# A two-layer mixture-of-experts trunk on one core: later gathers as transpositions by permutations, and the activations turned inside the next up product

## What is computed

```python
probs = softmax(t @ w_router)                    # 256 tokens, 16 experts in 4 groups of 4
# the best group by the sum of its two best scores; of that group the two best experts
gate = (one_hot(idx) * w).sum(1)                 # weight of each token for each expert, 14 of 16 zero
for e in range(16):
    g, u = split(t @ w_gu[e], 2)                 # 1024 -> 2 x 512
    out += gate[:, e] * ((silu(g) * u) @ w_down[e])   # 512 -> 1024
```

## Time and profile before

| | us |
|---|---|
| median of 3 runs | 721.49 (720.32 to 723.93) |
| profiled execution, its time | 720.53 |
| its span in the trace | 718.8 |
| TensorE busy | 678.9 |
| VectorE busy | 180.7 |
| ScalarE busy | 141.2 |
| GpSimd busy | 22.6 |

### The profile page before, as it was taken

How to read it: one execution, slowest core, us unless ns; L and a number is a source line. 1 busy time by engine, 2 the same in 40 slices (tenths; PEclk the granted TensorE clock), 3 DMA queues, 4 the chain that set the end, 5 groups by cost and what they waited for, 6 DMA issues and landing times.

```text
span 718.8 us, 7132 instructions
## 1 busy us (share of the span) xinstructions
PE 678.9 (94%) x2910; PEld 309.4 (43%) x2910; DVE 180.7 (25%) x452; ACT 141.2 (20%) x320; POOL 22.6 (3%) x41
## 2 busy tenths in 40 slices
PE   6999999999999999999989998999999999999983
PEld 5854564554343343433334455455333343343331
DVE  0010221460121121111135255553112112112125
ACT  1120360112121121211132051212111111121112
POOL 3200100000000000000000011200000000000000
PEclk9999999999999999999999999999999999999997
DMA  9999705145999999999999802650999999999921
GB/s 281 370 420 421 331 1 233 42 193 215 426 421 421 421 421 420 423 420 421 418 415 420 351 1 92 259 225 31 395 422 421 420 421 420 423 421 420 421 121 59
DMA packets 42165, 231.41 MB, mean 322 GB/s; under 512 B 8073, under 2 KB 12169, under 8 KB 16530
## 3 DMA queue, kind: packets, MB, share of 16 engines
q1 hardware_dynamic: 37696, 230.70, 78.4%
q10 hardware_dynamic: 4434, 0.21, 0.5%
HBM read 229.85 MB, written 1.05 MB: 321 GB/s over the span
## 4 chain that ended last, share of the span: by engine, by line
PE 88%; DVE 6%; ACT 3%; POOL 1%; ACTq 1%; issue 1%; POOLq 0%; DVEq 0%
PE pb L559 31%; PE pb L387 17%; PE pb L594 16%; PE pb L544 5%; PE pb L424 4%; PE pb L606 4%; PE pb L723 2%; PE pb L578 1%; PE pb L358 1%; PE pb L516 1%; PE pb L365 1%; DVE bufA L1255 1%; PE pb L525 1%; POOL bufA L339 1%; DVE bufA L1080 1%
## 5 line engine op out<-in xcount | busy, mean ns | idle before, releaser
L387 PE MATMUL pb<-ring,hT 128*128 128x512 f32 x320 | 141.3, 595 | 0.8 <-DVE hT L1409 0.8
L594 PE MATMUL pb<-ring,bufC 128*64 128x512 f32 x512 | 116.6, 597 | 7.2 <-DVE bufC L1246 7.2
L559 PE MATMUL pb<-ring,bufB 128*64 128x512 f32 x512 | 113.3, 595 | 1.9 <-DVE bufC L1242 1.9
L559 PE MATMUL pb<-ring,hT 128*64 128x512 f32 x512 | 113.0, 594 | 0.0
L387 PEld LDWEIGHTS pb<-ring,hT 128*128 128x128 f32 x320 | 59.5, 190 | 70.7 <-issue 68.7
L1255 DVE COPY bufA<-pb 32x512 f32<-32x512 f32 x64 | 43.7, 683 | 128.6 <-PE pb L594 128.1
L1242 DVE TENSOR_TENSOR bufC<-bufC,pb 128x256 f32<-128x256 f32 x32 | 13.5, 421 | 213.6 <-ACT bufC L953 213.6
L559 PEld LDWEIGHTS pb<-ring,hT 128*64 128x64 f32 x512 | 36.1, 137 | 69.7 <-issue 69.2
L594 PEld LDWEIGHTS pb<-ring,bufC 128*64 128x64 f32 x512 | 34.4, 136 | 73.3 <-issue 62.8
L559 PEld LDWEIGHTS pb<-ring,bufB 128*64 128x64 f32 x512 | 35.5, 137 | 70.3 <-issue 65.4
L947 ACT ACTIVATE bufA<-pb 32x512 f32<-32x512 f32 x64 | 37.7, 590 | 133.2 <-PE pb L594 132.8
(11 more groups left out here) (194 smaller groups left out, 410.6 us busy)
## 6 DMA issues: line engine op xcount, KB each, us to landing
ring<-in_w_gu SPq DMA_DIRECT2D x128, 1024.0 KB, 20.8
ring<-in_w_down SPq DMA_DIRECT2D x64, 1024.0 KB, 20.7
ring<-in_w_in_a SPq DMA_DIRECT2D x8, 1024.0 KB, 20.0
ring<-in_w_in_a SPq DMA_DIRECT2D x8, 512.0 KB, 10.5
ring<-in_w_out_a SPq DMA_DIRECT2D x4, 1024.0 KB, 18.9
ring<-in_w_q_b SPq DMA_DIRECT2D x4, 1024.0 KB, 23.9
ring<-in_w_out_b SPq DMA_DIRECT2D x4, 1024.0 KB, 23.6
ring<-in_w_kv_shared SPq DMA_DIRECT2D x2, 1024.0 KB, 27.6
```

What stands on the lines that cost most here:

```text
L387: last = mm(pb[bank][:, :], hT[:, k, t * P:(t + 1) * P], slot(i0 + k // 2)[0][:, k % 2, c * HALF:(c + 1) * HALF], start=k == 0, stop=k == ...
L559: last = mm(pb[0][c * 64:(c + 1) * 64, :].rearrange("p (a n) -> p a n", a=2), xe[m % 2][:, k, g * SLOTS:(g + 1) * SLOTS], slot(u_gu(l, u) ...
L594: last = mm(pb[2][c * 64:(c + 1) * 64, :], heT[:, j * P + hf * 64:j * P + (hf + 1) * 64], w[:, j, c * HALF:(c + 1) * HALF], start=(j, hf) ...
```

## The change

- In quads 2 to 4 a gather is four transpositions with the slot table in the place of the identity. The table is then a full permutation: `make_perm` compares lane numbers with a destination `dest` for every token of the tile, and a token that the quad does not have goes to one of the slots that nobody has. Its gate weight there is zero.
- `make_dest` computes the destinations, once a layer, after `count_rounds`; `route` saves the counts, capped at 32, for it. GpSimd fills three more constants. Some small tiles are joined in `misc`.
- `inner_T(u - 1)` is issued in the middle of `gate_up(u)`, before k = 4, and no longer after it; the last one of a layer stays behind the down product before it. On VectorE `take_T(u)` stands ahead of `times_up(u + 1)` instead of behind it.

```diff
-        ones = sb("ones", [P, 1])
+        misc = sb("misc", [P, 8])
+        ones, token_no, b_gate, extra_f = misc[:, 0:1], misc[:, 1:2], misc[0:GW, 2:3], misc[:, 4:8]
...
+        lane_no = sb("lane_no", [P, P])
+        block_no = sb("block_no", [P, EXPERTS])
+        count = st[:, 0:64]
+        d_free, d_sum, d_step, d_in = [st[:, 64 + 8 * n:72 + 8 * n].rearrange("p (m t) -> p m t", t=NT) for n in range(4)]
+        d_old = st[:, 128:160]
+        dest = sb("dest", [P, QUADS, NT])
...
-        NCONST = 8
+        NCONST = 11
...
             for t in range(NT):
                 nc.gpsimd.iota(slot_no[...]).then_inc(consts, 1)
+            nc.gpsimd.iota(lane_no[:, :], pattern=[[1, P]], ...).then_inc(consts, 1)
+            nc.gpsimd.iota(token_no[:, :], pattern=[[0, 1]], base=0, channel_multiplier=1, ...).then_inc(consts, 1)
+            nc.gpsimd.iota(block_no[:, :], pattern=[[BLOCK, GROUPS], [0, PER_GROUP]], ...).then_inc(consts, 1)
             nc.gpsimd.memset(w_gate, 0.0).then_inc(gate_zero, 1)
...
 def gather(m, f, bank=1):
-                        last = mm(pb[bank][:, (k % 4) * P:(k % 4 + 1) * P], rows_of(h, t, k),
-                                  pick[m % 2][:, t, :, :].rearrange("p e s -> p (e s)"), start=True, stop=True)
+                        to, table = pb[bank][:, (k % 4) * P:(k % 4 + 1) * P], pick[m % 2][:, t, :, :].rearrange("p e s -> p (e s)")
+                        if m:
+                            last = nc.tensor.transpose(to, rows_of(h, t, k), table)
+                        else:
+                            last = mm(to, rows_of(h, t, k), table, start=True, stop=True)
 def gate_up(u):
                     for k in range(KC):
+                        if u and k == 4:
+                            inner_T(u - 1)
...
                     gate_up(u + 1)
-                    inner_T(u)
                     if m:
                         scatter(m - 1)
                     down(u)
                     if more:
                         gather(m + 1, 0)
                     gate_up(u + 2)
-                    inner_T(u + 1)
                     if more:
                         gather(m + 1, 1)
                     down(u + 1)
                     if more:
                         gather(m + 1, 2)
                     gate_up(u + 3)
-                    inner_T(u + 2)
                     if more:
                         gather(m + 1, 3)
                     down(u + 2)
-                    inner_T(u + 3)
                     if more:
                         gate_up(u + 4)
                     else:
+                        inner_T(u + 3)
                         pe.wait_ge(x_sb, (Q0 + QUADS) * 4 - 3 * START)
                         bcast_row(1, 2 * l + 1, 0)
                     down(u + 3)
...
 def route(l):
                 V.reduce_max(extra_f[:, 0:1], pb[1][:, 32:64], AX_X)
+                V.tensor_scalar(count, pb[1][:, 0:64], float(BLOCK), None, ALU.min)
                 link(V.tensor_scalar(pt, r_a, 1.0, None, ALU.subtract))
...
+            def make_dest():
+                by_expert = lambda ap: ap.rearrange("p (t g i) -> p i t g", g=GROUPS, i=QUADS)
+                passed, total = by_expert(count[:, 0:32]), by_expert(count[:, 32:64])
+                pt = pos[:, :, :].rearrange("p e t -> p t e")
+                old = d_old.rearrange("p (t e) -> p t e", t=NT)
+                kept = r_a
+                V.tensor_reduce(d_sum, passed, AX_X, ALU.add)
+                V.tensor_tensor(old, pt, block_no[...], ALU.add)
+                link(V.scalar_tensor_tensor(out=kept, in0=kept, scalar=float(BLOCK), in1=oh, op0=ALU.is_le, op1=ALU.mult))
+                V.scalar_tensor_tensor(out=d_free, in0=total[:, :, :, 0], scalar=token_no[:, 0:1], in1=d_sum,
+                                       op0=ALU.add, op1=ALU.subtract)
+                link(V.tensor_tensor(old, old, kept, ALU.mult))
+                V.tensor_reduce(d_in, by_expert(d_old), AX_X, ALU.add)
+                for g in range(1, GROUPS):
+                    link(V.scalar_tensor_tensor(out=d_step, in0=d_free, scalar=float(g * BLOCK), in1=total[:, :, :, g],
+                                                op0=ALU.is_ge, op1=ALU.mult))
+                    link(V.tensor_tensor(d_free, d_free, d_step, ALU.add))
+                link(V.tensor_reduce(d_sum, by_expert(st[:, 96:128]), AX_X, ALU.add))
+                link(V.scalar_tensor_tensor(out=d_step, in0=d_sum, scalar=1.0, in1=d_free, op0=ALU.subtract, op1=ALU.mult))
+                link(V.tensor_tensor(dest[:, :, :], d_in, d_step, ALU.subtract))
+            def make_perm(m):
+                return V.tensor_tensor(pick[m % 2].rearrange("p t e s -> p t (e s)"),
+                                       lane_no[...].to_broadcast([P, NT, P]),
+                                       dest[:, m, :]...to_broadcast([P, NT, P]), ALU.is_equal)
...
                 make_pick(0).then_inc(pick_ready, 1)
                 count_rounds(l)
+                make_dest()
...
                     make_pickg(m).then_inc(pickg_ready, 1)
                     if more:
-                        make_pick(m + 1).then_inc(pick_ready, 1)
+                        make_perm(m + 1).then_inc(pick_ready, 1)
+                    take_T(u)
                     times_up(u + 1)
-                    take_T(u)
                     take_y(u)
+                    take_T(u + 1)
                     times_up(u + 2)
-                    take_T(u + 1)
                     take_y(u + 1)
+                    take_T(u + 2)
                     times_up(u + 3)
-                    take_T(u + 2)
                     take_y(u + 2)
                     take_T(u + 3)
```

More of the change, by code:

```diff
@@ L83, in build @@
         sink = sb("sink", [P, A_HEADS // 2])
-        b_gate = sb("b_gate", [GW, 1])
         cs = sb("cs", [P, NT, DH])
@@ L137, in build @@
         pos = sb("pos", [P, EXPERTS, NT])
+        lane_no = sb("lane_no", [P, P])
+        block_no = sb("block_no", [P, EXPERTS])
         gate = sb("gate", [P, EXPERTS, NT])
-        extra_f = sb("extra_f", [P, 4])
         extra = sb("extra", [P, 2], I32)
         ln = st[:, 0:40].rearrange("p (t n) -> p t n", t=NT)
+        count = st[:, 0:64]
+        d_free, d_sum, d_step, d_in = [st[:, 64 + 8 * n:72 + 8 * n].rearrange("p (m t) -> p m t", t=NT) for n in range(4)]
+        d_old = st[:, 128:160]
+        dest = sb("dest", [P, QUADS, NT])
         pb = [ctx.enter_context(nc.psum_tensor(f"pb{n}", [P, HALF], F32)) for n in range(8)]
@@ L308, in _ @@
                                allow_small_or_imprecise_dtypes=True).then_inc(consts, 1)
+            nc.gpsimd.iota(lane_no[:, :], pattern=[[1, P]], base=0, channel_multiplier=0,
+                           allow_small_or_imprecise_dtypes=True).then_inc(consts, 1)
+            nc.gpsimd.iota(token_no[:, :], pattern=[[0, 1]], base=0, channel_multiplier=1,
+                           allow_small_or_imprecise_dtypes=True).then_inc(consts, 1)
+            nc.gpsimd.iota(block_no[:, :], pattern=[[BLOCK, GROUPS], [0, PER_GROUP]], base=0, channel_multiplier=0,
+                           allow_small_or_imprecise_dtypes=True).then_inc(consts, 1)
             nc.gpsimd.memset(w_gate, 0.0).then_inc(gate_zero, 1)
@@ L1226, in of_quad @@
                         .rearrange("p t (g o) -> p t g o", o=1).to_broadcast([P, NT, 4, BLOCK]))
+            def make_dest():
[5 more added lines that the diff above has]
+                V.tensor_reduce(d_sum, passed, AX_X, ALU.add)
+                V.tensor_tensor(old, pt, block_no[:, :].rearrange("p (t e) -> p t e", t=1).to_broadcast([P, NT, EXPERTS]), ALU.add)
+                link(V.scalar_tensor_tensor(out=kept, in0=kept, scalar=float(BLOCK), in1=oh, op0=ALU.is_le, op1=ALU.mult))
[12 more added lines that the diff above has]
+                return V.tensor_tensor(pick[m % 2].rearrange("p t e s -> p t (e s)"),
+                                       lane_no[:, :].rearrange("p (t s) -> p t s", t=1).to_broadcast([P, NT, P]),
+                                       dest[:, m, :].rearrange("p (t o) -> p t o", o=1).to_broadcast([P, NT, P]), ALU.is_equal)
             def make_pick(m):
```

## The result

The changed kernel takes 713.0 us (median of 4 runs, 710.85 to 713.45) beside 721.42 for the kernel before: a ratio of 0.9863, 95% interval 0.9843 to 0.9883. The forecast was 712.3 (708.5 to 717.0). The profiled execution took 712.84, its span is 711.1.

A forecast was written before the change was run, and what follows sets the result against it. TensorE's own instructions were taken to bound the expert stages. Savings of 10.0 us over both layers, less 0.38 for the count and 0.45 for the start, gave -9.2: 721.49 to 712.3 us, range 708.5 to 717.0.

The forecast's parts named there:

- The bound: Expert stages: time is TensorE's own instructions and few waits; 88% of the last-ending chain is TensorE work, no DMA.
- six switches: Steady quad of 51.65 us: six changes between 64-column pairs and full 128-column work, 0.35 us each.
- Gathers: Quads 2 to 4: transpositions make a gather 0.48 us instead of 0.94, saving 0.46, 12 times a layer, 5.52 us.
- The move: Turning activations inside the next up product: loses nine shared switches a layer, costing 3.15 us, but hides copies.
- three better places: Moved turning where no gather fills the gap: first down product saves 0.91 us, quad 4 twice 0.86.
- Its reason: Turnings cannot stay behind their up product: a gather shortened by 0.46 us would only uncover VectorE's copy.
- The weights: Ring loads at layer 1's end lead by 9 to 11 us; 4 or more remain, no load late.
- VectorE's table: New slot table after the round count: 15 small operations, about 3 us, hidden in VectorE's idle time.
- The count: Capped count on VectorE ahead of the first gather's positions: not hidden, at most 0.19 us a layer, 0.38 in all.
- The start: GpSimd's three index fills delay ScalarE's first DMAs: 0.45 us, bounds 0 and 1.0.
- the dearer switch inside a product: Rival: a switch inside a running up product costs more, at 0.9 us giving 729 us; chance 0.05.
- The clock: Rival: TensorE's clock falls to half in the expert stages; four falls would give 719 us; chance 0.03.

The follow-up runs named there:

- e4: The changed kernel with turnings placed beside gathers or scatters where possible, only the first of a layer staying inside an up product; 706.8 us, ratio 0.9775.
- e5: e4 with the gathers' switches shared too, calls moved behind the scatter or beside turnings, none between an up and its down product; 705.0 us, ratio 0.9739.
- e7: The changed kernel with one more transposition inside each up product, issued before k = 2, so each is interrupted twice; 727.3 us, ratio 1.0049.
- e1: The changed kernel with gathers of quads 2 to 4 as plain matmuls again, turning still inside the next up product; 724.7 us, ratio 1.0019.
- e3: The changed kernel with the turning back behind its up product, keeping VectorE's new order, copy of turned activations ahead of the silu product; 711.5 us, ratio 0.9843.
- e8: The changed kernel with a weight ring of 18 slots in place of 22; 721.4 us, ratio 0.9962 to the kernel before.
- e6: e5 with GpSimd's three new constant fills moved behind the clearing that ScalarE's first DMAs wait for; 701.4 us, ratio 0.9707.

## Why the prediction was right

- *The bound* and the reading of a quad (six switches at 0.35, instructions at 0.117) held: the forecast quad was 50.86 and is 50.85, and e4, e5 and e7 found the same 0.35 with switches shared, shared further, and added.
- *Gathers*: 0.46 saved each was forecast; 0.4625 by e1. The Trainium skill's glossary in "TensorE: Matmul & The Clock Gate", with a factor of four for the transposition mode in float32, does not describe these gathers: their four transpositions take half the time of the eight instructions before.
- *The move*: nine lost switches and three better places were forecast at -3.15 + 2.63 a layer. e1 has +0.41 a layer beside before, forecast +0.52; its steady quad is 1.05 longer, three switches to the hundredth, and the 0.1 that is missing lies in quad 1. First product 0.85 saved for 0.91, last quad 2 x 0.85 for 2 x 0.86.
- *A layer*: 5.00 forecast, 5.14 measured.
- *Its reason*: here a step failed, though no number hung on it. I wrote that the turning "cannot stay where they are", since the copy would be uncovered. What stood in the way was the copy's place behind the silu product on VectorE, and the change had altered that too. e3 shows that the order alone is worth more than the move.
- *The weights*: a lead of 9 to 11 was read, with 4 or more to remain; 10.2 and 5.4 were found, and e8, which takes 10 us of it away and gives most of the gain back, shows that it was needed.
- *VectorE's table*: 3 us forecast, 2.7 measured, hidden. *The count*: 0.19 forecast, 0.13. *The start*: 0.45 forecast; 0.43 in ScalarE's first DMA, not to be told apart later.
- *The sum*: the forecast for the median is 0.7 too low. The stages gave 10.3 for 10.0. That the total came so near is in part luck: outside the stages the two traces differ by 2.6 us where start and count were to cost 0.8, and the forecast gain of 9.2 stands beside 7.7 by the profiled executions, 8.4 and 9.4 by two pairs of medians, and 9.9 by the ratio. The stretches at half clock were in the range for this; the 1.7 us put down for one is about the top of what they cost between the stages (0.6 to 1.6).
- *The rivals*: the dearer switch inside a product is out (0.59 with two transpositions, inside a product in the changed kernel and between products in e4). The clock was 1.00 in the expert stages in all traces, also in e5, where turning and gather stand together. The Trainium skill's "TensorE: Matmul & The Clock Gate", Part 4, says that transpositions do not count as busy in the same way as matmuls; no run here shows whether they do, and it cost nothing in these stages.

## What to carry to other kernels

Count the switches between kinds of work on TensorE and price one from a steady stretch; then give every small step a neighbour that pays the switch anyway, and half a product to hide its copy (e5 and e6: 2.6 and 2.9% under the kernel before, where the change had 1.4). Before moving a step to cover a late copy, look at what stands ahead of that copy on its own engine. And where compute outruns the DMA on a full ring, reckon the lead at the end of the stage: it bounds what any further saving can bring. In e5, with 1.5 us left, little more can be had from TensorE's work before the ring comes late.

## What was not expected

The length of a kernel's expert stage repeats to 0.02 us over chips, and over variants that leave the stage alone, while the medians of one kernel lie up to 2.4 us apart between sessions (721.4, 723.0, 723.8, 722.7 for the kernel before). For an edit inside such a stage one trace tells 0.1 us, where the medians of five rounds carry an interval of 1 to 2 us either way. And the first expert stage of the kernel before started at 166.5, 169.4 and 171.1 us in three traces (one with 18 slots), with half-clock stretches that fell differently in each.
